# Rotary pieces ordered one slot ahead of their transposes, with two buffers, and the first half of the mix split over four slots

## The reference, cut to what matters

```python
h = rms_norm(x, norm1_g)
proj = h @ w_in
qa, ka, va, qb, kb, vb, gb = split(proj)
y_a = swa_gqa_sinks(qa, ka, va, sinks, rel_bias)      # 8 heads of 64, window of chunks, softmax with a sink
qr = rotary(qb)                                       # 4 heads of 128
kr = rotary(kb) * 128 ** -0.5
o_b = chunkwise_retention(qr, kr, vb)                 # decay inside and across chunks
y_b = silu(gb) * head_group_norm(o_b, ret_gn_g)
x = x + concat([y_a, y_b]) @ w_out
h2 = rms_norm(x, norm2_g)
x = x + hierarchical_moe(h2, ...)                     # top-1 group, top-2 of 4 experts, 16 experts in all
return rms_norm(x, final_norm_g)

def rotary(t):                                        # halves t1, t2 of each head
    return concat([t1 * cos - t2 * sin, t1 * sin + t2 * cos], axis=-1)
```

## Time and profile before

| what | value |
|---|---|
| time, median of 3 runs | 566.18 us (565.38 to 569.23) |
| the profiled execution | 566.31 us |
| its span, first to last instruction | 564.2 us |
| PE busy | 542.2 us (96%) |
| DVE, ACT, POOL busy | 422.4 us (75%), 354.3 us (63%), 122.0 us (22%) |
| mean granted TensorE clock | 0.991 of full speed |

### The profile page before, as it was taken

The page is one execution under the profiler, slowest core; times in us unless marked ns, Lnnn a source line. Parts: engine busy times, 40 slices in busy tenths (PEclk is TensorE's granted clock), DMA queues, the critical chain, the costliest instruction groups (busy, mean ns, idle before and its releaser), DMA issues.

```text
span 564.2 us, 7883 instructions
## 1 busy us (share of the span) xinstructions
PE 542.2 (96%) x2679; PEld 440.0 (78%) x2680; DVE 422.4 (75%) x574; ACT 354.3 (63%) x472; POOL 122.0 (22%) x109
## 2 busy tenths in 40 slices
PE   4999979999999999998999999999999999999995
PEld 4988757777877888876888888888888888888883
DVE  3664588564864753476988898889888898888986
ACT  5563545761326253433778877888788788788754
POOL 2360000000000000012442344333442334420420
PEclk9999999999999999997999999999999999999998
DMA  8999112323020237768999999999999999999595
GB/s 293 375 307 384 30 64 76 74 76 70 6 76 0 76 112 261 235 249 280 353 375 371 371 373 387 364 346 366 358 384 359 362 367 380 378 367 379 133 210 182
DMA packets 71963, 144.02 MB, mean 255 GB/s; under 512 B 3784, under 2 KB 13312, under 8 KB 71808
## 3 DMA queue, kind: packets, MB, share of 16 engines
q1 hardware_dynamic: 64816, 120.77, 61.6%
q0 software_dynamic: 7120, 22.90, 13.5%
HBM read 132.77 MB, written 14.30 MB: 261 GB/s over the span
## 4 chain that ended last, share of the span: by engine, by line
PE 88%; DVE 5%; ACT 3%; DMA 2%; issue 2%; POOL 0%; POOLq 0%; DVEq 0%
PE ps L1434 25%; PE ps L1436 24%; PE ps L1435 24%; PE ps L1441 7%; PE ps L1583 2%; PE ps L1569 2%; PE ps L1546 1%; PE ps L1608 1%; DMA arena<-norm_g 1%; PE ps L1519 1%; ACT arena L736 1%; DMA arena<-h_dram,meta 1%; PE ps L1449 1%; PE ps L1454 1%; ACT hi_ring L678 1%
## 5 line engine op out<-in xcount | busy, mean ns | idle before, releaser
L1200 DVE TENSOR_TENSOR lo_ring<-arena,hi_ring 128x2048 fp32r<-128x2048 f32 x94 | 215.2, 2292 | 29.9 <-ACT hi_ring L859 28.8
L1434 PE MATMUL ps<-hi_ring,act_hi 128*128 128x512 f32 x576 | 232.7, 404 | 0.2 <-DVE act_lo L1126 0.2
L1436 PE MATMUL ps<-hi_ring,act_lo 128*128 128x512 f32 x576 | 225.5, 392 | 0.0
L1435 PE MATMUL ps<-lo_ring,act_hi 128*128 128x512 f32 x576 | 225.0, 391 | 0.0
L859 ACT ACTIVATE hi_ring<-arena 128x2048 fp32r<-128x2048 f32 x94 | 180.2, 1917 | 21.5 <-PE ps L1436 21.5
L1434 PEld LDWEIGHTS ps<-hi_ring,act_hi 128*128 128x128 f32 x576 | 108.7, 189 | 26.7 <-issue 6.0
L1436 PEld LDWEIGHTS ps<-hi_ring,act_lo 128*128 128x128 f32 x576 | 108.4, 188 | 23.6
L1435 PEld LDWEIGHTS ps<-lo_ring,act_hi 128*128 128x128 f32 x576 | 108.7, 189 | 20.2
L969 DVE SCALAR_TENSOR_TENSOR lo_ring<-arena,over,hi_ring 128x512 fp32r<-128x512 f32 x40 | 29.4, 749 | 33.5 <-ACT hi_ring L678 33.3
L581 POOL DMA_INDIRECT y_dram<-y,row_info x14 | 15.2, 1087 | 134.3 <-issue 134.3
L979 DVE TENSOR_TENSOR act_lo<-ps,act_hi 128x512 fp32r<-128x512 f32 x56 | 36.9, 684 | 7.9 <-ACT act_hi L708 5.0
(11 more groups left out here) (229 smaller groups left out, 533.1 us busy)
## 6 DMA issues: line engine op xcount, KB each, us to landing
arena<-w_gate SPq DMA_DIRECT2D x32, 1024.0 KB, 14.9
arena<-w_up SPq DMA_DIRECT2D x32, 1024.0 KB, 15.5
arena<-w_down SPq DMA_DIRECT2D x32, 1024.0 KB, 14.7
arena<-w_in SPq DMA_DIRECT2D x16, 512.0 KB, 11.5
y_dram<-arena POOLq DMA_DIRECT2D x8, 512.0 KB, 11.5
res<-y_dram POOLq DMA_DIRECT2D x8, 512.0 KB, 9.7
arena<-w_in SPq DMA_DIRECT2D x3, 1024.0 KB, 12.7
res<-x SPq DMA_DIRECT2D x4, 512.0 KB, 8.1
```

Of the source, the lines that this page charges most:

```text
L1200: nc.vector.tensor_tensor(lo(N1 + n12), raw(n12), hi(N1 + n12).bitcast(F32), ALU.subtract).then_inc(lo_done, 1)
L1434: nc.tensor.matmul(dst, a_hi, b_hi, start=start, stop=False)
L1435: nc.tensor.matmul(dst, a_hi, b_lo, start=False, stop=False)
L1436: return nc.tensor.matmul(dst, a_lo, b_hi, start=False, stop=stop)
```

## The change

Three things change. The rotations of pieces 0 to 3 move on VectorE from slots 4, 5, 7, 9 to 5, 7, 7, 9, and their transposes on TensorE and copies on ScalarE from slots 5, 7, 9, 11 to 6, 8, 10, 12. They get a second buffer (pieces 1 and 3 go into the first 512 columns of the mix's tile 2, which the attention writes in slot 14), so that a rotation waits only for the transposes of the piece two before it. The transposes use bank 7 in place of bank 4: the waits between them and the scores go, and waits between them and the transposes of the probabilities come (`turn_rot` for `pt_copied`, `turn_prob` for `rot_copied`). And the first half of the mix is split tile by tile over slots 28 to 31.

```diff
-ROTATE_SLOTS = (4, 5, 7, 9, 20, 22, 23, 25)
-ROT_SLOTS = (5, 7, 9, 11, 22, 23, 25, 26)
-ROT_BANKS = (4, 4, 4, 4, 5, 6, 5, 6)
+ROTATE_SLOTS = (5, 7, 7, 9, 20, 22, 23, 25)
+ROT_SLOTS = (6, 8, 10, 12, 22, 23, 25, 26)
+ROT_BANKS = (7, 7, 7, 7, 5, 6, 5, 6)
...
-MIX_A_SLOT, MIX_B_SLOT = 28, 35
+MIX_A_SLOTS, MIX_B_SLOT = (28, 29, 30, 31), 35
...
-        rot = region(O_ROT, 512)
+        rot = [region(O_ROT, 512), region(O_MIX + 2 * D, 512)]
...
-            def mix_hi(part):
+            def mix_hi(part, tiles=range(T)):
...
-                for t in range(T):
+                for t in tiles:
...
-                if k == MIX_A_SLOT:
-                    mix_hi(0)
+                if k in MIX_A_SLOTS:
+                    mix_hi(0, [t])
...
-                    if half == 0:
-                        ins.then_inc(score_read, 1)
...
-                ra = rot.rearrange("p (h a c) -> p h a c", a=2, c=B_DIM // 2)
+                own = rot[n % 2 if n < T else 0]
+                ra = own.rearrange("p (h a c) -> p h a c", a=2, c=B_DIM // 2)
...
                 if n:
-                    dve.wait_ge(rot_turned, n)
+                    dve.wait_ge(rot_ready, n)
+                if n >= 2:
+                    dve.wait_ge(rot_turned, n if n >= T else n - 1)
...
-                if k in ROTATE_SLOTS:
-                    rotate(ROTATE_SLOTS.index(k))
+                for n, slot in enumerate(ROTATE_SLOTS):
+                    if slot == k:
+                        rotate(n)
...
-                if k == MIX_A_SLOT:
-                    mix_lo(0)
+                if k in MIX_A_SLOTS:
+                    mix_lo(0, [t])
...
             def scores(u):
...
-                turned = sum(slot < SCORE_SLOTS[u] for slot in ROT_SLOTS[:T])
-                if turned:
-                    pe.wait_ge(rot_copied, turned)
...
             def turn_prob(u):
...
+                turned = sum(slot < TURN_SLOTS[u] for slot in ROT_SLOTS[:T])
+                if turned:
+                    pe.wait_ge(rot_copied, turned)
...
             def turn_rot(n):
                 pe.wait_ge(rot_ready, n + 1)
                 if n < T:
-                    pe.wait_ge(score_read, SCORE_SLOTS.index(ROT_SLOTS[n] - 1) + 1)
+                    pe.wait_ge(pt_copied, probs_value(TURN_SLOTS.index(ROT_SLOTS[n] - 1)))
...
-                turn(ROT_BANKS[n], [rot[:, i * P:(i + 1) * P] for i in range(4)]).then_inc(rot_turned, 1)
+                own = rot[n % 2 if n < T else 0]
+                turn(ROT_BANKS[n], [own[:, i * P:(i + 1) * P] for i in range(4)]).then_inc(rot_turned, 1)
```

More of the change, by code:

```diff
@@ L285, in build @@
             sem(n) for n in ("s_ready", "logit_ready", "exp_done", "p_turned", "pt_copied", "o_ready", "mix_a"))
-        sink_exp, p_scaled, score_read = sem("sink_exp"), sem("p_scaled"), sem("score_read")
+        sink_exp, p_scaled = sem("sink_exp"), sem("p_scaled")
         rot_ready, rot_turned, rot_copied = sem("rot_ready"), sem("rot_turned"), sem("rot_copied")
@@ L1076, in rotate @@
                 v8 = ps[:, t, :].rearrange("p (h c) -> p h c", c=64)
-                nc.vector.tensor_tensor(rot.rearrange("p (h c) -> p h c", c=64), v8, cs, ALU.mult)
+                nc.vector.tensor_tensor(own.rearrange("p (h c) -> p h c", c=64), v8, cs, ALU.mult)
                 step_done(nc.vector.tensor_tensor(rot_b.rearrange("p (h c) -> p h c", c=64), v8, sn, ALU.mult))
@@ L1120, in retention_out, with mix_lo @@
                                         ALU.mult).then_inc(mix_b, 1)
-            def mix_lo(part):
-                for t in range(T):
+            def mix_lo(part, tiles=range(T)):
+                for t in tiles:
                     rows = ps[:, 4 + t, :] if part else mix[:, t, 0:512]
```

## The result

| | before | after |
|---|---|---|
| median of 20 executions | 566.61 us (565.29 to 569.37) | 563.45 us (562.18 to 566.06) |
| span of the profiled execution | 564.2 us | 561.1 us |
| mean granted clock | 0.991 | 0.991 |

The ratio is 0.9944, with a 95% interval from 0.9927 to 0.9962: 3.2 us less by the medians, within 1%. Executions of one and the same kernel lie up to 4 us apart; that the clock does not fall at the same places in each is one reason, and the experiments come back to it.

What follows compares the result with a forecast made beforehand. TensorE's own work was taken as the bound (88% of the chain), so only its work or waits win time: 566.3 less 3.2 us for slot 5, nothing for the rest, gave 563.1 us, range 561.8 to 565.8, within 1%.

Steps and rivals of the forecast that it cites:

- Part 1, the stall in slot 5: Slot 5: TensorE's 3.03 us wait for rotation 0 goes, 3.2 us less, with 0.9 us spare before turn_rot(0).
- Part 2, what is late next: Slot 9: turn_prob(3), behind two rotations in VectorE's slot 7, is tightest, 0.3 us spare; no wait taken.
- Part 3, the rest moves along: From slot 6 on everything comes earlier by the same amount; transfers give back nothing.
- Part 4, the mix: Slots 28 to 31: splitting the mix's first half costs nothing and gains at most 0.5 us; taken as nothing.
- What a gap costs beside itself: TensorE's waits in slot 5 and at the gather: removing the first gives back no clock; the sum stays 3.2 us.
- The rival of the clock behind the gather: At the gather: half clock disappears, 559.7 us (chance 0.04), or lasts twice as long, 566.5 us (0.05).
- VectorE as the bound: Rival, slots 5 to 13: VectorE bounds them, TensorE waits 3 x 2.0 us from slot 8 to 11, 569.1 us; chance 0.03.
- a transfer that uses up the gain: Rival, later in the program: a transfer uses up the whole 3.2 us, leaving 566.3 us; chance 0.05.

Runs made afterwards that it cites:

- e3: The kernel before with two buffers for the rotations and nothing else moved: 566.58 us (one execution).
- e4: The changed kernel with one rotation buffer, each rotation waiting until the piece before it is turned: 566.06 us, ratio to before 0.998.
- e5: The changed kernel with VectorE's rotations ordered in slots 4, 5, 7, 9 again: 564.25 us (one execution).
- e6: The changed kernel with three unused additions (2.1 us) on VectorE behind the two rotations of slot 7: 563.87 us, ratio to before 0.995.
- e7: The changed kernel with three unused additions (2.1 us) on VectorE in slot 10: 559.83 us (one execution).
- e2: The changed kernel with the mix's first half back in slot 28: 563.35 us, ratio to before 0.9938.
- e1: The kernel before with only the mix's first half split over slots 28 to 31: 565.67 us, ratio to before 0.9986.
- e11: The kernel before with 24 in place of 14 filling matmuls before the gather's wait, e9 run again: 565.73 us, ratio to before 0.9963.
- e9: The kernel before with 24 in place of 14 filling matmuls before the gather's wait: 565.63 us, ratio to before 0.9981.
- e12: The changed kernel with 24 in place of 14 filling matmuls before the gather's wait, e8 run again: 560.58 us, ratio to before 0.9878.
- e8: The changed kernel with 24 in place of 14 filling matmuls before the gather's wait: 561.16 us, ratio to before 0.9893.

## Why the prediction was right, and where it was not

- *Part 1, the stall in slot 5*: right. From `turn_prob(1)` to `turn_prob(2)` the prediction had 8.50 us, measured are 8.40 (78.76 - 70.36); to `turn_prob(3)` 16.39 against 16.28. The room of 0.9 us in front of `turn_rot(0)` is there (75.49 - 74.59). e3, e4 and e5 show that TensorE's place, with the second buffer, does it, as the sum assumed.
- *Part 2, what is late next*: the place was right, slot 9, and the wait that was taken as nothing is nothing. The size of the room was not: 0.3 by the sums, none by e6. VectorE's side held, 14.64 us from 71.85 to 86.49 against 14.60. TensorE came 0.1 earlier than summed, and I let the signal arrive in no time, though TensorE starts 0.15 behind the division's end. Behind slot 9 there is room, as said (e7). That the second buffer is needed was not worked out; e4 gives its price, 4.2 us of the middle.
- *Part 3, the rest moves along*: right for the transfers. The rest is 311.9 after 311.8, with the clock falling at the gather in both profiles.
- *Part 4, the mix*: right, nothing (e2).
- *What a gap costs beside itself*: this step failed. "By these rows taking the first gap away gives back no clock" held for the one execution that I had a profile of. In others of the same wait (e1, e11) the clock was granted at 0.57 and 0.65 behind it, and filling the wait brought 1.1 to 1.7 us, so the term that the prediction put at nothing for the first gap is not nothing. The Trainium skill's rule (TensorE: Matmul & The Clock Gate, Part 1: The HAM clock gate), that the window runs free of the kernel, fits what the traces show: the same wait of 3.0 us stood before 1.00 in three kernels' profiles (before, e3, e9) and before half clock in two. No run here shows the window itself.
- *The rival of the clock behind the gather* was real, and in the forecast a matter of 9 in 100; its price, 3.4 by the windows, came to 2.8 in the rest. It explains a part of the scatter. Of 86 executions of the kernel before, taken beside the experiments, the 34 with a mean clock of 0.993 or more took 565.3 us on the average and the 23 with 0.989 or less 568.7. It does not explain the scatter after the change: 15 executions with the same mean clock of 0.991 lie 3.6 us apart (562.50 to 566.06).
- *The gain itself* depends on the clock too: with the gather filled on both sides the change is worth 5.1 us by the medians (e11 less e12), 4.5 by the means, where plain kernels show 3.2 and 3.5. What the change wins on the clock in slot 6 it seems to lose again at the gather. All five profiles with half clock there have a mean clock of 0.991; 0.992 or less came in 19 of the 20 executions after the change, and in 52 of the 86 of the kernel before. That is a rough sign only, since 2 of the 24 executions of e9 and e11, where the gather is filled, have 0.991 as well. So that 3.2 came out as forecast is in part luck: the sum had one term too few on either side, and the median of the kernel before by itself lay between 566.1 and 568.5 in five series.
- *VectorE as the bound, a transfer that uses up the gain*: neither came.

## What to carry to other kernels

Where an engine waits for a piece that was ordered in the very step before, move the use back by a step and give the piece a second buffer; here either one alone was worth nothing. Then look for the next late piece, and measure its room by putting a load of known size in front of it: slot 9 had none. And a wait of TensorE can have two prices, its length and, in a part of the executions, the clock behind it; where the wait itself cannot go, matmuls that nobody reads can bring back the second. One profile does not tell how often the clock falls: compare the mean clocks of many executions, and in a profile the time between two landmarks.

## What the runs showed of the hardware

- A wait of TensorE of 2.3 to 3.0 us may or may not be followed by half clock (1.2 GHz). It was after 3.03 in e1 and 3.02 in e11 (0.57 and 0.65 over the next four microseconds) and after 2.27 in e6 (0.61). It was not in e4, whose waits were 1.56 and 2.27, nor after the same 3.0 us in three other profiles (before, e3, e9). It cost 1.2 to 1.7 us of the middle.
- The same holds at the gather: half clock came after waits of 2.2 to 2.5 us in five profiles (before, after, e2, e3, e5), and none after 2.2 to 2.4 us in four (e1, e4, e6, e7).
- Half clock behind the gather costs 2.8 us of the rest. With ten more matmuls of filling neither profile (e8, e12) shows it, and all 12 executions have a mean clock of 0.996 to 0.998, where the five profiles with half clock there have 0.991.
- No profile here shows half clock both in slots 6 to 10 and behind the gather. The mean clocks suggest that it happens: 0.989 or less came in 23 of 86 executions of the kernel before, 3 of 12 of e1 and 3 of 10 of e6, all with a wait of over 2 us in slots 5 to 9 and with the gather as it was, and in none after the change (20) or in e2 (12), nor with the gather filled in e8 to e12 (48). Against it, none of the 10 of e4 is so low, in spite of its waits of 1.56 and 2.27.
- The start of the kernel, up to the first scores, scatters by 2.4 us (52.8 to 55.2) with nothing changed in it. What moves it was not tried.
